# Routing gates of a two-block transformer: the gated one-hots built token by token on VectorE, the squares of the other one-hots shared by ScalarE and GpSimd

## The reference, cut to what matters

```python
expert = jnp.take_along_axis(cand_id, pos, axis=-1)
gate = jax.nn.softmax(top_s, axis=-1)
# for each token t, head h, choice k:
act = jax.nn.gelu(jnp.einsum('thkd,td->thk', ug, xc).astype(jnp.float32), approximate=False)
w = (gc * act).astype(vg.dtype)
return jnp.einsum('thk,thkd->td', w, vg)
```

## Time and profile before

| | us |
|---|---|
| median of 3 runs | 1792.36 |
| lowest, highest | 1786.25, 1793.43 |
| the profiled execution, own time | 1799.46 |
| its span, first to last instruction | 1797.6 |
| gates stage, from the first one-hot (621.8) to the end of the last L2038 (743.1) | 121.3 |

### The profile page before, as it was taken

One profiled execution on the slowest core, in us unless ns is written; L12 is line 12 of the kernel. 1 busy time (PEld: TensorE's weight loads), 2 busy tenths in 40 slices (PEclk: granted clock), 3 DMA queues, 4 the chain that ended last, 5 costly groups with the idle time before them and its releaser, 6 DMA issues.

```text
span 1797.6 us, 31061 instructions
## 1 busy us (share of the span) xinstructions
PE 1699.4 (95%) x9982; PEld 1429.1 (80%) x9982; DVE 1262.7 (70%) x2545; ACT 1020.1 (57%) x2016; POOL 77.2 (4%) x74
## 2 busy tenths in 40 slices
PE   7898999999999888899999999988999999899997
PEld 6764998888888655688888888966888879888886
DVE  5446559989996699866666676457676666767666
ACT  5444556666666688555555554337565555446553
POOL 0000000000000165200000000000000000000000
PEclk9989999999999899999999999999999999999999
DMA  6545445555555588555565654410365554545552
GB/s 236 195 153 175 152 154 188 180 188 185 185 187 186 198 279 284 193 192 195 191 219 190 196 190 150 161 36 1 112 199 190 190 199 147 158 142 191 192 188 94
DMA packets 86935, 316.34 MB, mean 176 GB/s; under 512 B 9664, under 2 KB 9808, under 8 KB 86352
## 3 DMA queue, kind: packets, MB, share of 16 engines
q1 hardware_dynamic: 85248, 309.30, 51.6%
q10 hardware_dynamic: 1328, 4.01, 0.6%
q0 software_dynamic: 288, 2.10, 0.3%
HBM read 314.32 MB, written 1.05 MB: 175 GB/s over the span
## 4 chain that ended last, share of the span: by engine, by line
PE 89%; DVE 5%; ACT 2%; issue 2%; DMA 2%; POOLq 0%; ACTq 0%; DVEq 0%
PE acc L495 21%; PE bank L505 20%; PE bank L495 11%; PE acc L496 10%; PE bank L506 10%; PE bank L496 5%; PE bank L884 4%; PE acc L606 3%; PE bank L627 1%; DMA route<-in_ada_w 1%; ACT arena L1141 1%; DVE small L2176 1%; PE bank L846 0%; DVE w_lo L1665 0%; ACT L1141 0%
## 5 line engine op out<-in xcount | busy, mean ns | idle before, releaser
L1665 DVE TENSOR_TENSOR w_lo<-raw,w_hi 128x512 fp32r<-128x512 f32 x982 | 667.4, 690 | 413.2 <-ACT w_hi L1141 410.9
L1141 ACT ACTIVATE w_hi<-raw 128x512 fp32r<-128x512 f32 x982 | 614.8, 632 | 549.3 <-PE acc L495 252.8
L505 PE MATMUL bank<-x_both,w_hi 128*128 128x512 f32 x1532 | 544.2, 400 | 2.8 <-DVE x_both L2288 2.8
L506 PE MATMUL bank<-x_both,w_lo 128*128 128x256 f32 x1532 | 430.9, 281 | 0.0
L505 PEld LDWEIGHTS bank<-x_both,w_hi 128*128 128x128 f32 x1532 | 288.6, 188 | 75.5 <-issue 3.2
L506 PEld LDWEIGHTS bank<-x_both,w_lo 128*128 128x128 f32 x1532 | 290.2, 189 | 0.5
L495 PE MATMUL bank<-x_both,w_hi 128*128 128x256 f32 x1384 | 256.1, 287 | 14.3 <-DVE w_lo L1665 10.2
L495 PEld LDWEIGHTS bank<-x_both,w_hi 128*128 128x128 f32 x1384 | 218.7, 194 | 19.4 <-issue 10.5
L495 PE MATMUL acc<-w_hi,x_both 128*128 128x512 f32 x560 | 219.6, 392 | 3.9 <-DVE w_lo L1665 2.5
L495 PE MATMUL acc<-w_lo,x_both 128*128 128x512 f32 x560 | 218.9, 391 | 0.0
L496 PE MATMUL acc<-w_hi,x_both 128*128 128x512 f32 x560 | 218.9, 391 | 0.0
(11 more groups left out here) (260 smaller groups left out, 1824.4 us busy)
## 6 DMA issues: line engine op xcount, KB each, us to landing
raw<-in_peer_u SPq DMA_DIRECT2D x128, 512.0 KB, 3.5
raw<-in_peer_v SPq DMA_DIRECT2D x128, 512.0 KB, 4.2
raw<-in_mlp_w SPq DMA_DIRECT2D x128, 512.0 KB, 3.5
ada_x<-in_ada_w SPq DMA_DIRECT2D x64, 512.0 KB, 4.2
route<-in_ada_w SPq DMA_DIRECT2D x32, 512.0 KB, 6.0
raw<-in_w_in SPq DMA_DIRECT2D x25, 512.0 KB, 4.5
raw<-in_conv_w_in SPq DMA_DIRECT2D x24, 512.0 KB, 4.3
raw<-in_attn_w_in SPq DMA_DIRECT2D x18, 512.0 KB, 3.5
```

Of the source, the lines that this page charges most:

```text
L505: first = mm(ps[:, :], w[0], x_joined[:, :, c * T:(c + 1) * T], start=(c == 0), stop=False, **kw)
L506: return first, mm(ps[:, 0:T], w[1], x_hi[:, c * T:(c + 1) * T], start=False, stop=(c == KC - 1), **kw)
L1141: return nc.scalar.activation(dst, src, f, **kw)
L1665: v.tensor_tensor(w_lo[:, unit(n, half)], raw[:, a:a + HALF], w_hi[:, unit(n, half)].bitcast(F32), ALU.subtract).then_inc(s["lo_done"], 1)
```

## The change

VectorE no longer compares four tokens with one instruction and leaves the gates to GpSimd. It makes the gated one-hot of each token with one instruction of 128 x 128: iota is compared with the token's column of `iT`, and the result multiplied by its column of `gT`, both of them per-partition scalars read from SBUF. It signals `gated_i` itself; `eq_i` and `one_jd` are gone. The two `jone` compares of VectorE in each round are gone as well. ScalarE now does the relu for all eight groups, and the squares for groups 0, 2, 3, 5 and 6. GpSimd does the squares for groups 1, 4 and 7 with two instructions of 128 x 512: iota - j, then the difference times itself, with a wait of its own between the two (`j_diff`). It starts when the relu of the group two before is done, and ScalarE waits for it by `j_sq_pool`.

```diff
-J_ACT = (0, 1, 2, 4, 5, 6)
+J_POOL = (1, 4, 7)
+J_ACT = (0, 2, 3, 5, 6)
...
 # TensorE
-                    if g in J_ACT:
-                        pe.wait_ge(s["one_j"], i * len(J_ACT) + (J_ACT.index(g) + 1))
-                    else:
-                        pe.wait_ge(s["one_jd"], i * 2 + (n + 1))
+                    pe.wait_ge(s["one_j"], i * 8 + (g + 1))
                     pe.wait_ge(s["gated_i"], i * 8 + (g + 1))
...
 # ScalarE
+            def one_hot_j(g, i=0):
+
+                if g in J_ACT:
+                    act.wait_ge(s["j_sq"], i * len(J_ACT) + (J_ACT.index(g) + 1))
+                else:
+                    act.wait_ge(s["j_sq_pool"], i * len(J_POOL) + (J_POOL.index(g) + 1))
...
+            def one_hots_j(groups, i=0, last=False):
+
+                for g in groups:
+                    if not (last and g == 7):
+                        if g:
+                            act.wait_ge(s["one_j"], i * 8 + g)
+                        squares(g + 1, i)
+                    one_hot_j(g, i)
...
 # GpSimd
-            with pool.Fori(0, 8) as i:
-                for g in range(8):
-                    pool.wait_ge(s["eq_i"], i * 8 + (g + 1))
-                    e = ione[:, (g % 4) * 512:(g % 4 + 1) * 512].rearrange("p (t k) -> p t k", t=4)
-                    nc.gpsimd.tensor_tensor(e, e, gT[:, bass.ds(i * 32 + 4 * g, 4)].unsqueeze(2).to_broadcast([P, 4, P]),
-                                            ALU.mult).then_inc(s["gated_i"], 1)
+            def squares(g, turn, i=0):
+
+                shape = [P, 4, P]
+                d = jsq[:, g % 2 * 512:(g % 2 + 1) * 512]
+                nc.gpsimd.tensor_tensor(d.rearrange("p (t k) -> p t k", t=4), C("iota").unsqueeze(1).to_broadcast(shape),
+                                        jT[:, bass.ds(i * 32 + 4 * g, 4)].unsqueeze(2).to_broadcast(shape),
+                                        ALU.subtract).then_inc(s["j_diff"], 1)
+                pool.wait_ge(s["j_diff"], i * len(J_POOL) + turn)
+                nc.gpsimd.tensor_tensor(d, d, d, ALU.mult).then_inc(s["j_sq_pool"], 1)
...
+            with pool.Fori(1, 8) as i:
+                for n, g in enumerate(J_POOL):
+                    pool.wait_ge(s["one_j"], i * 8 + (g - 1))
+                    squares(g, n + 1, i)
...
 # VectorE
+            def gated_one_hot(g, token):
+
+                for t in range(4):
+                    a = g % 4 * 512 + t * P
+                    last = v.tensor_scalar(ione[:, a:a + P], C("iota"), iT[:, bass.ds(token + t, 1)], gT[:, bass.ds(token + t, 1)],
+                                           ALU.is_equal, ALU.mult)
+                last.then_inc(s["gated_i"], 1)
...
             with dve.Fori(0, 8) as i:
                 for g in range(8):
-                    one_hot_i(g + 3, i * 32 + 4 * (g + 3))
-                    if g % 4 == 2:
-                        one_hot(jone[:, 512:1024], jT, i * 32 + 4 * (g + 1)).then_inc(s["one_jd"], 1)
-
+                    gated_one_hot(g + 3, i * 32 + 4 * (g + 3))
                     wait_full(dve, "g", g, i * 2)
```

More of the change, by code:

```diff
@@ L113 @@
     exps_ready qk_gla_ready at_zeroed moba_sq_ready head_rstd
-    moba_tables sm1_max sm1_exp sm1_p moba_o_full sq2_ready route_done gate_exp gate_ready eq_i one_j one_jd j_sq
+    moba_tables sm1_max sm1_exp sm1_p moba_o_full sq2_ready route_done gate_exp gate_ready one_j j_sq j_diff j_sq_pool
     gated_i silu_c mod_ready v_full gated_hi gated_lo lam_in attn_v_full attn_v_ready b_sq b_rstd b_rope
@@ L1380, in _, with squares @@
             wait_full(act, "u", ROUND - 1, 2 * (TILE["u"][1] // ROUND - 1))
[L1382 to L1396, removed]
+            def squares(g, i=0):
+                if g % 8 in J_ACT:
+                    for t in range(4):
+                        a = g % 2 * 512 + t * P
+                        last = fn(jsq[:, a:a + P], C("iota"), ACT.Square, bias=njT[:, bass.ds(i * 32 + (4 * g + t), 1)])
+                    last.then_inc(s["j_sq"], 1)
+            def one_hot_j(g, i=0):
[3 more added lines that the diff above has]
+                    act.wait_ge(s["j_sq_pool"], i * len(J_POOL) + (J_POOL.index(g) + 1))
                 b, turn = use("g", g - 2)
                 act.wait_ge(bank_full[b], i * 2 + (turn + 1))
-                fn(jone[:, (g % 2) * 512:(g % 2 + 1) * 512], jsq[:, (n % 2) * 512:(n % 2 + 1) * 512], ACT.Relu, scale=-1.0,
+                fn(jone[:, (g % 2) * 512:(g % 2 + 1) * 512], jsq[:, (g % 2) * 512:(g % 2 + 1) * 512], ACT.Relu, scale=-1.0,
                    bias=C("one")).then_inc(s["one_j"], 1)
+            def one_hots_j(groups, i=0, last=False):
[5 more added lines that the diff above has]
+                    one_hot_j(g, i)
             wait_freed(act, "route", 0)
@@ L1405, in _ @@
             squares(0)
[L1406 to L1417, removed]
+            one_hots_j(range(8))
+            with act.Fori(1, 7) as i:
+                act.wait_ge(s["one_j"], i * 8)
+                one_hots_j(range(8), i)
+            act.wait_ge(s["one_j"], 7 * 8)
+            one_hots_j(range(8), 7, last=True)
             ada_copy(1, acc[0])
@@ L1620, in _ @@
             nc.gpsimd.memset(at_sb, 0.0).then_inc(s["at_zeroed"], 1)
-            with pool.Fori(0, 8) as i:
-                for g in range(8):
-                    pool.wait_ge(s["eq_i"], i * 8 + (g + 1))
-                    e = ione[:, (g % 4) * 512:(g % 4 + 1) * 512].rearrange("p (t k) -> p t k", t=4)
-                    nc.gpsimd.tensor_tensor(e, e, gT[:, bass.ds(i * 32 + 4 * g, 4)].unsqueeze(2).to_broadcast([P, 4, P]),
-                                            ALU.mult).then_inc(s["gated_i"], 1)
+            def squares(g, turn, i=0):
[6 more added lines that the diff above has]
+                nc.gpsimd.tensor_tensor(d, d, d, ALU.mult).then_inc(s["j_sq_pool"], 1)
+            wait_freed(pool, "route", 0)
+            squares(1, 1)
+            for n in range(1, len(J_POOL)):
+                pool.wait_ge(s["one_j"], J_POOL[n] - 1)
+                squares(J_POOL[n], n + 1)
+            with pool.Fori(1, 8) as i:
+                for n, g in enumerate(J_POOL):
+                    pool.wait_ge(s["one_j"], i * 8 + (g - 1))
+                    squares(g, n + 1, i)
             pool.wait_ge(s["v_full"], 7)
@@ L2017, in _ @@
             v.tensor_tensor(lamw[:, 1:2], V("lam", 2), V("lam", 3), ALU.mult).then_inc(s["lam_in"], 1)
[L2019 to L2026, removed]
+            def gated_one_hot(g, token):
+                for t in range(4):
+                    a = g % 4 * 512 + t * P
+                    last = v.tensor_scalar(ione[:, a:a + P], C("iota"), iT[:, bass.ds(token + t, 1)], gT[:, bass.ds(token + t, 1)],
+                                           ALU.is_equal, ALU.mult)
+                last.then_inc(s["gated_i"], 1)
             for g in range(3):
-                one_hot_i(g, 4 * g)
+                gated_one_hot(g, 4 * g)
             with dve.Fori(0, 8) as i:
                 for g in range(8):
-                    one_hot_i(g + 3, i * 32 + 4 * (g + 3))
-                    if g % 4 == 2:
-                        one_hot(jone[:, 512:1024], jT, i * 32 + 4 * (g + 1)).then_inc(s["one_jd"], 1)
+                    gated_one_hot(g + 3, i * 32 + 4 * (g + 3))
                     wait_full(dve, "g", g, i * 2)
```

## The result

| | before | changed |
|---|---|---|
| median, us | 1789.74 (4 runs) | 1813.6 (4 runs) |
| lowest to highest | 1786.25 to 1793.43 | 1810.84 to 1814.22 |
| profiled execution, own time (span) | 1799.46 (1797.6) | 1814.22 (1812.3) |
| gates stage in it, first one-hot to end of last product | 121.3 | 143.5 |

The ratio is 1.0123, 95% interval 1.0102 to 1.0143: 22 us slower. In the two traces the gates stage is 22.2 us longer (613.3 to 756.8 instead of 621.8 to 743.1). Behind it both take the same, 1055.5 and 1054.5 us. Ahead of it the profiled execution of the changed kernel was 8.5 us shorter, in code that is the same; in the traces of all kernels of this study the stage's first one-hot lies between 613 and 622 us, so this is scatter.

A forecast was written before the change was run, and what follows sets the result against it. VectorE was taken to set the gates stage's pace: 13.3 us of its own work plus 4.2 lost to GpSimd make 17.5 us a round against 14.77, 22 us over eight rounds, so 1792.4 + 22 = 1814 us; range 1788 to 1832.

The forecast's parts named there:

- Part 1: Gates stage, VectorE: 32 gated one-hots at 0.26 us, 8.3 us a round; with products 13.3, against 11.0 before.
- The bound by ScalarE's squares: High end for one gated one-hot on VectorE: 0.32 us, from ScalarE's four squares in 1.28 us.
- Part 2: Gates stage: GpSimd's three pairs a round block VectorE's one-hots, 1.4 us lost per pair, 4.2 a round.
- Part 3: ScalarE, 12.7 us of work a round, waits for GpSimd: 14.3 us, no cost while VectorE needs 17.5.
- the circle: ScalarE's relu, GpSimd's pair and back to ScalarE: 3.4 us a stretch, 14.3 us a round (13.7 to 14.7).
- No waiting for GpSimd: Rival, chance 0.18: short one-hots don't wait for GpSimd; VectorE 13.3, relu and GpSimd last at 14.3 us a round; 1788.
- The whole gain: Rival, chance 0.03: GpSimd always in time, ScalarE's 12.7 us a round last; 17 us less in all, 1775.
- nothing for the end: Rival, chance 0.02: a round stays near 14.8 us by chance of phases, so the end doesn't move.
- The clock falls: Rival, chance 0.07: TensorE, busy 71%, loses full clock in a fifth of the stage; 12 us more, 1826.

The follow-up runs named there:

- wide instruction: Changed kernel, each group's four TENSOR_SCALAR replaced by one 512-column TENSOR_TENSOR with two SBUF inputs, comparison left out: 1789.03 us, ratio 0.9981 to the kernel before.

## Why the prediction was right, point by point

**The outcome.** 1814 was forecast, 1813.6 measured, inside 1788 to 1832. The forecast was made against a median of 1792.4, which a fourth run has brought to 1789.74; the change itself is 22 us by the ratio and 23.9 by the medians, 22 forecast. For the profiled execution 1821.5 was forecast and 1814.22 measured, since it had come to the stage 8.5 us earlier; the stage itself grew by 22.2. The round is 17.5 us, as forecast; but two terms in it were wrong and cancelled, and that part is luck, as is the agreement of the medians to 0.4 us when the four runs before span 7.

**Part 1 held.** A one-hot starts every 0.255 us (0.26 forecast, from rows with another width and the right number of scalars) and takes 0.336; VectorE's own work is 13.1 us a round, 13.3 forecast. The bound by ScalarE's squares, 0.32, wasn't needed: the addresses cost nothing visible. The short estimate by the Trainium skill ("VectorE: DVE Perf Modes", The TRN2 errata), 0.13 us for one, is refuted by the trace; the same section says itself that this row comes out short, of a copy of 2048 elements.

**Part 2 held in its mechanism and its sum, not in its parts.** That the one-hots wait for GpSimd was the assumption on which all rested; three runs show it: no GpSimd, no long one-hots; a quarter of the width, a small loss; one input in PSUM, none. The Trainium skill ("SBUF — State Buffer", SBUF: two separate sides) says this of a two-port instruction, and the trace now agrees for TENSOR_SCALAR of fp32: up to 1.221 us instead of 0.336. The loss was forecast as 1.4 us a pair. Measured: 23 of the 24 pairs lie behind the first product, and (137.9 - 63 x (4 x 0.255 + 0.62)) / 23 = 1.50. But I had GpSimd's square at 1.26 us, by the earlier trace rows, and it takes 1.04, so a pair holds 1.78 us and not 2.0; and I let one product of 0.62 us hide in each pair. A typical pair lies wholly on one set of four one-hots and costs 1.59 (above). It starts when ScalarE's relu ends, and by then VectorE is in the one-hots; a product helps only in a few pairs. So the hold was taken too long by 0.22 us, and what products hide too large by some 0.3: 0.28 of 1.78, and not 0.62 of 2.0.

**Part 3 held.** ScalarE waits 0.3 us in all for GpSimd, since VectorE's 17.5 us cover the circle. That the circle exists shows where VectorE is relieved (wide instruction: 11.0 us of waits, a round of 14.4 us). The 14.3 forecast for it had the square at 1.26 us; there both instructions of a pair took 1.21, held up by VectorE.

**The rivals.** *No waiting for GpSimd* would have been 14.3 us a round and is out by the long one-hots themselves. *The whole gain* and *nothing for the end* are out by the time. *The clock falls*: it does a little, to 0.89 in one of six stretches in the middle, though not in the five others, where TensorE is busy for 66 to 76% and the rival had it at 71%; but a round doesn't end by TensorE, and VectorE stays at 100%. It was priced as if TensorE would become last, and costs nothing here. Its condition, more than one slow round in a row, wasn't met.

**What stays open.** Why a pair of a quarter of the width costs 0.10 us on the mean and not 0.5; I gave one reading of it above, and no run tests that alone. And how much of a GpSimd instruction shuts VectorE out: the 0.89 us of 1.04 are worked out from two places of the trace before, and no run varied them.

## What to carry to other kernels

When VectorE and GpSimd work side by side, ask of each VectorE instruction what it reads: two SBUF tensors, or one in the fast two-way mode, make it wait for GpSimd and GpSimd for it; with iota in PSUM neither waited, in both forms measured here. A constant that is compared or multiplied again and again can lie in a free PSUM bank, which freed VectorE of 3.0 us a round in the kernel before (from 14.1 without its waits to 11.1; the round kept 0.9 of it, since TensorE came next) and cost nothing (one-hots of 512 columns) or 0.07 us (128 columns in the two-way mode). And giving one wide instruction's work to four narrow ones costs a fixed part each time, which rows with the same number of scalar operands tell in advance.

## What the runs showed of the hardware that I had not expected

- GpSimd multiplies two full inputs in 1.04 us when both are the same tensor (24 instructions, 1038 to 1040 ns). With two different ones it takes 1.26, a product (L1637 before) as well as the sum in the earlier trace rows; with a broadcast input 1.04. With 128 columns instead of 512 it takes 0.40.
- A VectorE instruction with one PSUM input and a GpSimd instruction leave each other alone to a few ns: compares of 512 columns 659 to 691 ns over 83 instructions, GpSimd 1035 to 1046 over 64.
- Reading 128 fp32 columns from PSUM instead of SBUF made a TENSOR_SCALAR 0.067 us longer (0.403 instead of 0.336), which is what 64 columns take at the rate of the compares (512 in 0.54): the two-way mode had saved half of the 128. It isn't a fixed price of reading PSUM: with 256 columns and one scalar the difference is 0.128 us, twice as much, between the line below and the 0.352 us of L1741 from SBUF, both of the kernel before.

```profile
L1723 DVE TENSOR_SCALAR arena<-bank,vec x2: 476/480/483, 35.3 to 35.7; 128x256 f32<-128x256 f32 x2
```
